# Sixteen experts unrolled: the down product one expert later, low parts of the weights in halves on VectorE, weighting on ScalarE, neighbouring weight rows in one partition

## What is computed

```python
def expert_choice_ffn(h, w_router, w_gate, w_up, w_down):
    ...
    gate, idx = lax.top_k(jnp.swapaxes(aff, 1, 2), cap)
    xg = h[bidx, idx]
    g = jnp.einsum('becd,edf->becf', xg, w_gate)
    u = jnp.einsum('becd,edf->becf', xg, w_up)
    y = jnp.einsum('becf,efd->becd', jax.nn.silu(g) * u, w_down) * gate[..., None].astype(h.dtype)
    return jnp.zeros_like(h).at[bidx, idx].add(y)
```

## Time and profile before

| | before |
|---|---|
| time, median of 3 | 3798.75 us (3797.96 to 3799.34) |
| the profiled execution: time, span | 3797.84 us, 3796.1 us |
| mean granted TensorE clock | 0.942 |
| PE busy | 3405.8 us, 90% of the span |
| PEld, DVE, ACT, POOL busy | 73%, 37%, 29%, 36% |
| DMA, mean over the span | 90 GB/s |

### The profile page before, as it was taken

How to read it: one execution, slowest core, us unless ns; L and a number is a source line. 1 busy time by engine, 2 the same in 40 slices (tenths; PEclk the granted TensorE clock), 3 DMA queues, 4 the chain that set the end, 5 groups by cost and what they waited for, 6 DMA issues and landing times. The chain is left out here.

```text
span 3796.1 us, 45430 instructions
## 1 busy us (share of the span) xinstructions
PE 3405.8 (90%) x16792; PEld 2786.7 (73%) x16792; DVE 1406.7 (37%) x1980; ACT 1089.7 (29%) x1647; POOL 1364.6 (36%) x644
## 2 busy tenths in 40 slices
PE   4888995768688868999999899999999999999988
PEld 3677884655466656778787688878888888888877
DVE  4664224643676655321111332321222222222232
ACT  4264213422455522100110211101333332332332
POOL 2330321431555544333333444433333332333222
PEclk8999996889788879999999899999999999999999
DMA  7130104053789862132113211132221221121122
GB/s 231 25 90 30 43 17 137 0 180 120 237 292 304 298 179 62 50 111 64 45 39 99 68 50 50 44 116 67 40 45 33 39 45 39 39 39 39 39 56 83
DMA packets 410399, 340.22 MB, mean 90 GB/s; under 512 B 83526, under 2 KB 347514, under 8 KB 410178
## 3 DMA queue, kind: packets, MB, share of 16 engines
q1 hardware_dynamic: 335068, 300.73, 25.3%
q10 hardware_dynamic: 70630, 21.43, 2.6%
q0 software_dynamic: 4608, 16.78, 1.9%
HBM read 287.06 MB, written 48.43 MB: 88 GB/s over the span
## 5 line engine op out<-in xcount | busy, mean ns | idle before, releaser
L273 POOL TENSOR_TENSOR w_hi<-w_raw,zero_col 128x1024 fp32r<-128x1024 f32 x193 | 366.0, 1896 | 1650.9 <-PE first_z L308 640.6
L276 POOL TENSOR_TENSOR w_lo<-w_raw,w_hi 128x1024 fp32r<-128x1024 f32 x193 | 499.5, 2588 | 15.2
L308 PE MATMUL first_z<-h_hi,w_hi 128*128 128x512 f32 x1216 | 392.6, 404 | 4.4 <-DVE h_lo L2074 4.4
L308 PE MATMUL first_z<-h_lo,w_hi 128*128 128x512 f32 x1216 | 377.4, 392 | 0.0
L308 PE MATMUL first_z<-h_hi,w_lo 128*128 128x512 f32 x1216 | 375.6, 390 | 0.0
L308 PEld LDWEIGHTS first_z<-h_hi,w_lo 128*128 128x128 f32 x1216 | 228.8, 188 | 49.6
L308 PEld LDWEIGHTS first_z<-h_lo,w_hi 128*128 128x128 f32 x1216 | 228.9, 188 | 48.5
L308 PEld LDWEIGHTS first_z<-h_hi,w_hi 128*128 128x128 f32 x1216 | 220.2, 189 | 43.2 <-DVE h_lo L2074 4.5
L308 PE MATMUL dil_z<-h_hi,w_hi 128*128 128x512 f32 x640 | 219.1, 423 | 0.6 <-POOLq L264 0.6
L308 PE MATMUL dil_z<-h_lo,w_hi 128*128 128x512 f32 x640 | 199.8, 394 | 0.0
L3266 DVE SCALAR_TENSOR_TENSOR dil_biased<-const,dil_slope_now,dil_aux 128x128 f32<-128x128 f32 (+1 forms) x192 | 78.4, 409 | 322.7 <-PE dil_aux L3118 312.6
(11 more groups left out here) (564 smaller groups left out, 7042.6 us busy)
## 6 DMA issues: line engine op xcount, KB each, us to landing
w_raw<-in_odd_w_in SPq DMA_DIRECT2D x112, 512.0 KB, 3.7
raw_gate<-in_w_gate SPq DMA_DIRECT2D x16, 2048.0 KB, 8.4
raw_up<-in_w_up SPq DMA_DIRECT2D x16, 2048.0 KB, 9.9
raw_down<-in_w_down SPq DMA_DIRECT2D x16, 2048.0 KB, 7.6
w_raw<-in_even_w_in SPq DMA_DIRECT2D x40, 512.0 KB, 3.8
scan_w_mod<-in_w_mod SPq DMA_DIRECT2D x12, 1024.0 KB, 10.3
start_w_mod<-in_w_mod SPq DMA_DIRECT2D x8, 1024.0 KB, 10.9
w_raw<-in_w_in SPq DMA_DIRECT2D x16, 512.0 KB, 3.7
```

What stands on the lines that cost most here:

```text
L273: pool.tensor_tensor(w_hi[:, u], w_raw[:, u], zero_col[:, 0:1].to_broadcast([P, KT * P]).rearrange("p (k n) -> p k n", k=KT), ALU.add).the ...
L276: pool.tensor_tensor(w_lo[:, u], w_raw[:, u], w_hi[:, u].bitcast(F32), ALU.subtract).then_inc(self.split, 1)
L308: ins = pe.matmul(z, w[:, u, kt], rhs[:, kt, c0:c0 + width], start=first, stop=last)
```

## The change

- The weights lie in the partitions as `(p k)`: partition p has 8 neighbouring rows of gate and up, or 4 of down. The x rows and the gated product are read at strides of 8 and 4 words to match: block k of x then has the features 8p + k.
- The loops are unrolled over 17 rounds. In round e PE does gate(e), the f transposes of e - 1, up(e), the x transposes of e + 1 and down(e - 1).
- Low parts of all three weights are made by DVE in halves, the high parts by ACT in halves; PE waits for a half before the first matmul on it. Gate(e) waits for `x_hi` at its start and for `x_lo` only before its last eight matmuls.
- ACT weights the down product (`weigh`), two rounds after the expert's gate product, ahead of everything else in its round.
- POOL has only the indirect DMAs; they use the columns of `slot_token` directly, and four gathers are issued ahead. SP issues loads in the order gate, up, down of the expert before.

The diff, cut to its core:

```diff
-        exp_src = {w: A[f"w_{w}"].rearrange("o e (k p) n -> p (o e) k n", p=P) for w in EXP_SHAPES}
+        exp_src = {w: A[f"w_{w}"].rearrange("o e (p k) n -> p (o e) k n", p=P) for w in EXP_SHAPES}
...
+                    def load(w, e):
+                        sp.wait_ge(used[w], e - 1)
+                        sp.dma_start(raw[w, e % 2][:], exp_src[w][:, e]).then_inc(loaded[w, e % 2], 16)
+
+                    for e in range(2, E + 1):
+                        if e < E:
+                            load("gate", e)
+                            load("up", e)
+                        if e >= 3:
+                            load("down", e - 1)
...
-                    def lo_down(e, slot):
-                        pool.wait_ge(hi_done["down"], e + 1)
-                        pool.tensor_tensor(w_lo_["down", slot][:], raw["down", slot][:], w_hi_["down"][:].bitcast(F32), ALU.subtract).then_inc(split["down"], 1)
...
+                    for e in range(4):
+                        gather(e)
+                    for e in range(E):
+                        scatter(e)
+                        if e + 4 < E:
+                            gather(e + 4)
...
+                            ins = pe.transpose(p_x[:, kt // 4, (kt % 4) * P:(kt % 4 + 1) * P], xg[:, e % 2, :].rearrange("p (q k) -> p k q", k=KT)[:, kt, :], ident)
...
+                    for e in range(E + 1):
+                        if e < E:
+                            gate(e)
+                        if e:
+                            turn_f(e - 1)
+                        if e < E:
+                            up(e)
+                        if e + 1 < E:
+                            turn(e + 1)
+                        if e:
+                            down(e - 1)
...
+                    def weigh(e):
+                        act.wait_ge(used["down"], e + 1)
+                        if e >= 2:
+                            act.wait_ge(scattered, 16 * (e - 1))
+                        act.activation(y[:, e % 2, :], p_y[:].rearrange("p a b -> p (a b)"), ACT.Copy, scale=slot_gate[:, e:e + 1]).then_inc(y_out, 1)
+
+                    hi_x(0)
+                    for e in range(E + 1):
+                        if e >= 2:
+                            weigh(e - 2)
+                            hi("down", e - 1)
+                        if e:
+                            act.wait_ge(f_turned, e)
+                            act.copy(f_hi[:], p_f[:]).then_inc(f_hi_done, 1)
+                        if e < E:
+                            act.wait_ge(used["gate"], e + 1)
+                            if e:
+                                act.wait_ge(prod_done, e)
+                            act.activation(silu[:], p_gu[:, 0, :], ACT.Silu).then_inc(silu_done, 1)
+                        if e + 1 < E:
+                            hi("gate", e + 1)
+                            hi_x(e + 1)
+                            hi("up", e + 1)
+                    weigh(E - 1)
...
+                    for e in range(E + 1):
+                        if e >= 2:
+                            lo("down", e - 1, 0)
+                            lo("down", e - 1, 1)
+                        if e:
+                            dve.wait_ge(f_hi_done, e)
+                            dve.tensor_tensor(f_lo[:], p_f[:], f_hi[:].bitcast(F32), ALU.subtract).then_inc(f_lo_done, 1)
+                        if e + 1 < E:
+                            lo("gate", e + 1, 0)
+                        if e < E:
+                            dve.wait_ge(silu_done, e + 1)
+                            dve.wait_ge(used["up"], e + 1)
+                            if e:
+                                dve.wait_ge(f_turned, e)
+                            dve.tensor_tensor(prod[:], silu[:].rearrange("p (q k) -> p k q", k=FK), p_gu[:, 1, :].rearrange("p (q k) -> p k q", k=FK),
+                                              ALU.mult).then_inc(prod_done, 1)
+                        if e + 1 < E:
+                            lo("gate", e + 1, 1)
+                            lo_x(e + 1)
+                            lo("up", e + 1, 0)
+                            lo("up", e + 1, 1)
```

More of the change, by code:

```diff
@@ new lines, in gate @@
+                    def gate(e):
+                        pe.wait_ge(x_hi_done, e + 1)
+                        if e:
+                            pe.wait_ge(silu_done, e)
+                        for kt in range(KT):
+                            if e and kt % (KT // 2) == 0:
+                                pe.wait_ge(split["gate"], 2 * (e - 1) + kt // (KT // 2) + 1)
+                            pe.matmul(p_gu[:, 0, :], x_hi[:, e % 2, kt, :], w_hi_["gate"][:, kt, :], start=(kt == 0), stop=False)
+                            pe.matmul(p_gu[:, 0, :], x_hi[:, e % 2, kt, :], w_lo_["gate", e % 2][:, kt, :], start=False, stop=False)
@@ L2460, in run @@
-                    def run(e, slot, round_, last):
-                        pe.wait_ge(x_lo_done, e + 2)
-                        pe.wait_ge(prod_done, e + 1)
-                        for b, w in enumerate(("gate", "up")):
-                            pe.wait_ge(split[w], parts_of[w] * (e + 2))
-                            product(p_gu[:, b, :], w, slot, x_hi[:, slot], x_lo[:, slot], KT, slice(None)).then_inc(used[w], 1)
-                        if not last:
-                            turn(e + 1, 1 - slot, round_ + slot)
-                        pe.wait_ge(prod_done, e + 2)
-                        pe.wait_ge(f_lo_done, e + 1)
+                            ins = pe.matmul(p_gu[:, 0, :], x_lo[:, e % 2, kt, :], w_hi_["gate"][:, kt, :], start=False, stop=(kt == KT - 1))
@@ new lines, in gate, with up @@
+                        ins.then_inc(used["gate"], 1)
+                    def up(e):
+                        if e:
+                            pe.wait_ge(prod_done, e)
+                        for kt in range(KT):
+                            if e and kt % (KT // 2) == 0:
+                                pe.wait_ge(split["up"], 2 * (e - 1) + kt // (KT // 2) + 1)
+                            pe.matmul(p_gu[:, 1, :], x_hi[:, e % 2, kt, :], w_hi_["up"][:, kt, :], start=(kt == 0), stop=False)
+                            pe.matmul(p_gu[:, 1, :], x_hi[:, e % 2, kt, :], w_lo_["up", e % 2][:, kt, :], start=False, stop=False)
+                        for kt in range(KT):
+                            ins = pe.matmul(p_gu[:, 1, :], x_lo[:, e % 2, kt, :], w_hi_["up"][:, kt, :], start=False, stop=(kt == KT - 1))
+                        ins.then_inc(used["up"], 1)
@@ L2496, in run @@
-                    def run(e, slot, round_, last):
-                        act.wait_ge(used["gate"], e + 2)
-                        act.wait_ge(prod_done, e + 1)
-                        act.activation(silu[:], p_gu[:, 0, :], ACT.Silu).then_inc(silu_done, 1)
-                        if not last:
-                            hi("gate", e + 1, 1 - slot, round_ + slot)
-                        act.wait_ge(f_turned, e + 1)
-                        act.copy(f_hi[:], p_f[:]).then_inc(f_hi_done, 1)
-                        if not last:
-                            hi_x(e + 1, 1 - slot)
-                            hi("up", e + 1, 1 - slot, round_ + slot)
-                            hi("down", e + 1, 1 - slot, round_ + slot)
@@ L2509, in _, with hi @@
-                    for w in shapes:
-                        act.sem_inc(hi_done[w], parts_of[w])
-                    hi_x(0, 0)
-                    pairs(act, run)
+                    def hi(w, e):
+                        if e >= 2:
+                            act.wait_ge(loaded[w, e % 2], 16 * (e // 2))
+                        act.wait_ge(used[w], e)
+                        for kts in halves(w):
+                            act.copy(w_hi_[w][:, kts], raw[w, e % 2][:, kts]).then_inc(hi_done[w], 1)
```

183 lines of the change are left out of this document (53 added, 130 removed).

## The result

The changed kernel takes 3705.47 us (median of 4, 3697.71 to 3712.61) against 3799.05 us (median of 4) for the kernel before: a ratio of 0.9753, 95% interval 0.9733 to 0.9773, so 94 us faster. The profiled execution took 3706.18 us (span 3704.4).

What follows compares the result with a forecast made beforehand. Weight transfers, 20.6 us an expert against PE's 18.8, were to bound later experts: 997.9 + 14 x 20.6 + 4.1 + 3.7 + 12.6 = 1306.7 us for the last product, not 1376.6; gain 70, so 3728 us (range 3702 to 3754).

Steps and rivals of the forecast that it cites:

- Rival B: Expert stretch: PE sets the whole pace, last product at 1299.2 us, or 1282.2 with unslowed turns; 3704 to 3720 us; chance 0.18.
- T: DMA time per expert: three weight loads at 5.5 us plus 4.1 for gather and scatter, 20.6 us, from 18.8 to 22.0.
- the 22.0 us of today's floor: Transfers of one expert in the kernel before: 17.9 us weight queue plus 4.1 gather and scatter, from busy shares.
- the forecast's own chain: Expert stretch: first load issued at 997.9, then 14 T, 4.1, 3.7 and 12.6 us to the last product.
- Turns: Eight x transposes on PE, read at a stride: 2.0 us, double the 1.02, bounded between 1.0 and 4.1.
- Closing round: After down(14), the last expert's weighting, halves, f_lo, 16 matmuls and hand-overs: 12.6 us to the last product.
- the 5.0 + 1.3 us go: PE's period per expert: 5.0 us idle and 1.3 of low clock vanish with down one expert later.
- C: Weight loads: large packets gain nothing, T = 22.0 us, last product at 1326.3, 3748 us; chance 0.17.
- D: Weight queue: a 16 KB packet holds its engine 0.96 us, T = 27.1, slower, 3819 us; chance 0.04.
- E: x transposes on PE: turns at four times, PE has 20.8 us an expert, 3754 us; chance 0.06.
- F: Expert stretch: no change, the new order gives place to a wait as long, 3798 us; chance 0.03.

Runs made afterwards that it cites:

- e1: The changed kernel with the old weight layout, 2 and 4 KB packets, x turns and gated product contiguous again: 3717.0 us, ratio 0.9788.
- e7: The changed kernel without the scatters of the first 15 experts, only the last expert's output added: 3701.9 us, ratio 0.9747.
- e10: The changed kernel with 4 KB packets, x turns at a stride of 2 elements, gated product contiguous: 3708.7 us, ratio 0.9767.
- e3: The kernel before with only the low part of down moved, whole, from POOL to DVE, behind the weighting: 3720.9 us, ratio 0.9798.
- e5: The changed kernel with the low part of each down matrix given back to POOL, whole: 3780.2 us, ratio 0.9947.
- e9: The kernel before with the low part of down on DVE, the new layout and its loops written out: 3721.1 us, ratio 0.9801.
- e6: The changed kernel with the weighting back on DVE, at the head of its round: 3705.9 us, ratio 0.9763.
- e8: The changed kernel with high and low parts made whole, one instruction for each matrix, not in halves: 3708.3 us, ratio 0.9762.

## Why the prediction was right and wrong

**Right: direction, range, and what PE gets rid of.** No PE wait for the gated product, low halves at 2.29 us, POOL without tensor work, an eighth as many q1 packets for gate and up, the stretch after the experts unchanged. DVE has 16.3 us (predicted 16.3, the same by luck: the gated product was put at 0.67 us and takes 1.10, and neighbouring instructions overlap a little, 1106.83 + 1.10 against a next start at 1107.85) and ACT 14.1 (13.8, with weighting at 1.12 us where x_hi gave 1.02).

**Wrong: the likeliest time, 3728 us, by 22, and what was to set the later rounds.** The forecast (own range 3718 to 3738, chance 0.52) had PE waiting for weights, 2 us an expert; PE waited for none in the middle. Rival B with unslowed turns happened, 3704 us, last product at 1282.2 (measured 1285.6), to which I gave 0.18. The range of 3702 to 3754 holds 3705 only because it took in B, so the hit owes more to its width than to the forecast. Two terms of the sum failed, and a third was short.

*T, "3 x 5.5 + 4.1 = 20.6 us".* The step that the transfers are late next held, its size did not. Measured: 18.8 us, from landings that grow by 1.1 us an expert. The parts agree: 79.5% x 35.6 / 12.01 = 2.36 us per MB, 4.9 us for 2.1 MB, three times, and 22.0% x 35.6 / 2 = 3.9 for gather and scatter: 18.7. That is my lower bound (4.9, from the best slices); I took 5.5, from the 8 KB packets of the earlier trace rows. Those rows are a short load, 0.60 MB in 1.7 us, and may have the long packets of a head themselves; no run tests it. The error began with the 22.0 us of today's floor: e1 gives 19.5 with the very same packets. The sum of shares took as work the long packets of a short queue (e7): q1 takes 2.86 us per MB before (1050 to 1230: 73.0% of 180 us for 46.01 MB) and 2.63 in e1 (82.5%, 56.48 MB). And it took two queues for exclusive that overlap to a share of 1.04 (e1, 1138 to 1217 us).

With 18.8 the forecast's own chain gives 997.9 + 14 x 18.8 + 20.4 = 1281.5 and rival B's 1282.2. What B misses of 1285.6 is the start, gate(0) at 991.1 instead of 989.2, and the closing round below. So the two bounds meet, and the kernel stands where PE hides the transfers with nothing to spare. The Trainium skill's page DMA: Bandwidth & Descriptors, section Bandwidth, has 425 GB/s for a core alone, by which B would hold, as it did: 397 were measured with scatters among the loads, 418 in the middle of a load of e7.

*Turns, "take double, 2.0".* Measured 1.09 us for eight, against 1.02. A turn's weight load does take 192 ns instead of 140, but the next one starts before it ends, some 0.13 us apart as before. A price seen on DVE was carried to PE. On DVE it was real and smaller: 1.10 us for the gated product, not 1.35; it reads one operand in SBUF and one in PSUM at the stride, and which of them costs is not shown. The Trainium skill's page Advanced Engine Details and Errata, section SBUF Cachelines, has a penalty where each access meets another 16-byte line and full speed where accesses share one. Here a weight load is slower at either stride: 192 ns at 8 words, and 209 in e10 at 2 words, where two words share a line. It hardly touches PE's pace: eight turns take 1.09 and 1.15 us.

*Closing round, 12.6.* Measured from the last f turns at 1271.3 to 1285.6: 14.3. The clock is low after PE's wait of 5.2 us for f_hi, 0.50 from 1277.1 to 1282.4, which the term left out. PE's weight loads there, kernel after:

```profile
1277.11 0.29 PEld L2456 LDWEIGHTS exp_y<-hi_down,f_hi 128*128 128x128 f32 x1 [5.18 <-ACT f_hi L2503]
...
1279.25 0.29 PEld L2456 LDWEIGHTS exp_y<-hi_down,f_hi 128*128 128x128 f32 x1 [0.78 <-DVE lo_down L2520]
```

(The list of PE's waits above puts the same wait down to lo_down, as 5.0.)

**Right for an incomplete reason: "the 5.0 + 1.3 us go" with the later down product.** e3 and e5 split it. Taking the low part off POOL gives 78 us alone; everything but that (e5) gives 15. The order, with what goes with it, then gives the last 14 (e9), if the layout lets the transfers follow (e1). What the layout is worth depends on what else is there: a loss of 14 us alone, nothing in the time beside e3, a gain of 12 at the end. Weighting and unrolling are worth nothing measurable (e6, e9), the halves 7 us of the stretch (e8). The prediction had the held DVE half as the reason of the wait, but its sum credited the gain to the place of the down product.

**Rivals.** C (22.0), D (16 KB packet at 0.96 us; measured 79.5% x 35.6 x 16 / (12.01 / 0.01638) = 0.62 us) and E (turns at 4.1) are excluded by the rows above. F is excluded by the result.

**Open.** The first packets of a load last longer on an empty queue; in the kernel before some last longer in the middle of a gate load as well (1127 to 1131: 332 GB/s at a share of 100%), and why was not settled. The runs of the changed kernel spread over 10 to 15 us. Little of it seems to arise among the experts: the two traces of the changed kernel have gate(0) at 991.1 and 984.6 us, 294.5 and 294.8 from there to the last product, and 2418.8 and 2421.8 behind it. Why the other phases differ so was not settled.

## What to carry to other kernels

A transfer floor read from a queue's busy share came out too high here, where the queue was not backlogged (22.0 against 19.5 us with the same packets); take it from MB per us in a stretch where landings lengthen, or from the best slices. When DMA and PE are close, watch the landings grow from load to load: a floor above PE's period costs nothing while buffered lead lasts. A GpSimd tensor instruction beside a VectorE one with two SBUF inputs was paid twice here, by its own 9 us and by the 3 to 6 us for which it holds the other; look for that before reordering anything. When times of runs differ by a few us, compare the stretch that the change touches, from its own first instruction.

## What was unexpected of the hardware

- Issue of a load on SP takes 0.33 us in 16 KB packets whatever is queued, but 3.3 to 8.5 us in the 2 and 4 KB packets of e1 from 1090 us on, and up to 5.4 in the 4 KB packets of e10.
- How exactly the hold works: a VectorE half that starts beside GpSimd's low part ends 2.15 to 2.16 us after GpSimd does, in the kernel before and in e5.
- The strided gated product costs 1.10 us instead of 0.67, the strided weight load of a turn 192 ns instead of 140 (209 at a stride of 2 words, e10), while eight turns go only from 1.02 to 1.09 us (1.15 in e10).
